# A fused encoder block on one core: the first gate and up blocks of the second feed-forward layer in alternating fours of halves, and the last quarter of x turned by VectorE

## What is computed

```python
def rms_norm(x, w):
    y = xf * lax.rsqrt(jnp.mean(xf * xf, axis=-1, keepdims=True) + EPS)
    return (y * w)

def swiglu(h, w_gate, w_up, w_down):            # 2048 -> 5632 -> 2048
    return (jax.nn.silu(h @ w_gate) * (h @ w_up)) @ w_down

x = x + 0.5 * swiglu(rms_norm(x, norm_ffn1_w), ...)
x = x + head_group_mixer(rms_norm(x, norm_mix_w), ...)
x = x + 0.5 * swiglu(rms_norm(x, norm_ffn2_w), ...)
return rms_norm(x, norm_final_w)
```

## Time and profile before

| | us |
|---|---|
| median of three runs | 1797.8 |
| the profiled execution | 1797.76 |
| its span in the trace | 1795.9 |
| PE busy | 1786.4 |
| VectorE busy | 1271.0 |
| ScalarE busy | 811.8 |

### The profile page before, as it was taken

The page is one execution under the profiler, slowest core; times in us unless marked ns, Lnnn a source line. Parts: engine busy times, 40 slices in busy tenths (PEclk is TensorE's granted clock), DMA queues, the critical chain, the costliest instruction groups (busy, mean ns, idle before and its releaser), DMA issues.

```text
span 1795.9 us, 22263 instructions
## 1 busy us (share of the span) xinstructions
PE 1786.4 (99%) x8104; PEld 1476.3 (82%) x8104; DVE 1271.0 (71%) x1622; ACT 811.8 (45%) x976; POOL 59.2 (3%) x57
## 2 busy tenths in 40 slices
PE   9999999999999999999999999999999999999998
PEld 7888888888888888888888888888888888888886
DVE  6676676676676678688888786676676667667668
ACT  6434444444443444555455445443443443444444
POOL 0000000000000000002222000000000000000000
PEclk9999999999999999999999999999999999999999
DMA  9655565565555555555546456556556556655552
GB/s 382 206 187 190 198 195 187 190 199 195 187 191 199 193 187 193 182 168 190 183 163 211 141 181 217 193 199 193 187 192 200 192 187 192 200 192 187 193 200 97
DMA packets 175590, 346.66 MB, mean 193 GB/s; under 512 B 5952, under 2 KB 8640, under 8 KB 175424
## 3 DMA queue, kind: packets, MB, share of 16 engines
q1 hardware_dynamic: 174976, 345.35, 57.8%
q10 hardware_dynamic: 576, 0.81, 0.1%
HBM read 344.04 MB, written 2.10 MB: 193 GB/s over the span
## 4 chain that ended last, share of the span: by engine, by line
PE 98%; DMA 0%; ACT 0%; issue 0%; DVE 0%; SPq 0%; POOLq 0%; POOL 0%; DVEq 0%; ACTq 0%
PE ps L381 32%; PE ps L382 32%; PE ps L383 32%; PE ps L410 0%; DMA raw<-in_g 0%; PE ps L598 0%; PE ps L587 0%; PE ps L523 0%; PE ps L536 0%; ACT w_hi L656 0%; PE ps L487 0%; PE ps L486 0%; PE ps L485 0%; SPq L337 0%; ACT xT_hi L663 0%
## 5 line engine op out<-in xcount | busy, mean ns | idle before, releaser
L901 DVE TENSOR_TENSOR w_lo<-raw,w_hi 128x1024 fp32r<-128x1024 f32 x644 | 797.3, 1239 | 496.7 <-ACT w_hi L679 495.3
L679 ACT ACTIVATE w_hi<-raw 128x1024 fp32r<-128x1024 f32 x644 | 681.3, 1059 | 955.6 <-PE ps L383 948.8
L381 PE MATMUL ps<-w_hi,xT_hi 128*128 128x512 f32 (+1 forms) x1808 | 702.2, 388 | 0.3 <-DVE xT_lo L934 0.3
L382 PE MATMUL ps<-w_lo,xT_hi 128*128 128x512 f32 (+1 forms) x1808 | 700.2, 387 | 0.0
L383 PE MATMUL ps<-w_hi,xT_lo 128*128 128x512 f32 (+1 forms) x1808 | 700.0, 387 | 0.0
L381 PEld LDWEIGHTS ps<-w_hi,xT_hi 128*128 128x128 f32 x1808 | 339.5, 188 | 71.2 <-issue 1.4
L383 PEld LDWEIGHTS ps<-w_hi,xT_lo 128*128 128x128 f32 x1808 | 339.5, 188 | 69.6
L382 PEld LDWEIGHTS ps<-w_lo,xT_hi 128*128 128x128 f32 x1808 | 339.6, 188 | 68.5
L383 PE MATMUL ps<-w_hi,hT_lo 128*128 128x512 f32 x640 | 249.0, 389 | 0.0
L381 PE MATMUL ps<-w_hi,hT_hi 128*128 128x512 f32 x640 | 249.0, 389 | 0.0
L382 PE MATMUL ps<-w_lo,hT_hi 128*128 128x512 f32 x640 | 249.0, 389 | 0.0
(11 more groups left out here) (116 smaller groups left out, 540.0 us busy)
## 6 DMA issues: line engine op xcount, KB each, us to landing
raw<-in_u SPq DMA_DIRECT2D x88, 1024.0 KB, 5.1
raw<-in_d SPq DMA_DIRECT2D x88, 1024.0 KB, 4.9
raw<-in_g SPq DMA_DIRECT2D x85, 1024.0 KB, 5.1
raw<-in_w_in SPq DMA_DIRECT2D x40, 1024.0 KB, 4.9
raw<-in_w_out SPq DMA_DIRECT2D x16, 1024.0 KB, 5.0
raw<-in_g SPq DMA_DIRECT2D x4, 512.0 KB, 7.6
x<-in_x SPq DMA_DIRECT2D x4, 512.0 KB, 12.8
raw<-in_w_in SPq DMA_DIRECT2D x4, 512.0 KB, 3.7
```

What stands on the lines that cost most here:

```text
L381: pe.matmul(out, xh, wh, start=first and j == 0, stop=False)
L382: pe.matmul(out, xh, wl, start=False, stop=False)
L679: act.activation(w_hi[:, k % LEAD, :, 0:width], words[:, :, 0:width], ACT.Copy).then_inc(hi_ready, 1)
L901: dve.tensor_tensor(w_lo[:, k % LEAD, :, 0:width], words[:, :, 0:width], f32(w_hi[:, k % LEAD, :, 0:width]), ALU.subtract).then_inc(lo_rea ...
```

## The change

The first gate and up blocks of the second feed-forward layer are no longer computed one after the other. The 16 halves go in fours: gate with pairs 0 to 3, up with pairs 0 to 3, gate with pairs 4 to 7, up with pairs 4 to 7 (`first_both`). The loads follow that order. Gate is complete behind half 11, so SiLU moves to position 13. Pair 4 is first used by half 8 where it was half 4, pair 6 by half 10 where it was half 6.

Quarter 3 is turned by VectorE in place of PE, four pieces behind each of positions 2 to 5 (`FOURTH_X`), into PSUM banks 6 and 7. ScalarE and VectorE write their parts of pairs 6 and 7 together ahead of position 7 (`LATER_PARTS`).

```diff
-X_BY_DVE = [(FFN2, 0), (FFN2, 2)]
+X_BY_DVE = [(FFN2, 0), (FFN2, 2), (FFN2, 3)]
+FOURTH_X = {2: (0, 4), 3: (4, 8), 4: (8, 12), 5: (12, 16)}
+FIRST_PARTS = {1: (4,), 2: (5,), 3: (6,), 4: (7,)}
+LATER_PARTS = {1: (4,), 2: (5,), 7: (6, 7)}
...
         def x_bank(norm, p):
-            return (0, 1, 2, 3, 4, 5, 2, 3)[p]
+            return p if norm == FFN2 else (0, 1, 2, 3, 4, 5, 2, 3)[p]
...
                     for s in range(4):
-                        if 4 * part + s >= loaded:
+                        if f == 1 and isinstance(i, int):
+                            load(g + part, s, rows(ffn_w[f][s // 2], 4 * P * (2 * part + s % 2), i * W))
+                        elif 4 * part + s >= loaded:
                             load(g + part, s, rows(ffn_w[f][part], 4 * P * s, i * W))
...
                     half(g, k, xT_hi, xT_lo, 2 * k, bank, k == 0, k == 7)
-                    if norm == FFN2 and bank == B_GATE and k in (2, 3):
-                        turn_x(norm, k + 4)
+
+            def first_both(g):
+
+                for pos in range(16):
+                    p, bank = 4 * (pos // 8) + pos % 4, (B_GATE, B_UP)[pos % 8 // 4]
+                    if bank == B_GATE:
+                        pe.wait_ge(xT_lo_ready, PAIRS * FFN2 + p + 1)
+                    half(g + pos // 8, pos % 8, xT_hi, xT_lo, 2 * p, bank, p == 0, p == 7)
...
             def silu(f, g, i):
-                act.wait_ge(half_used, 8 * g + 8)
+                act.wait_ge(half_used, 8 * g + (12 if f == 1 and isinstance(i, int) else 8))
...
                 for k in range(16):
-                    if 1 <= k < 5:
-                        xT(norm, k + 3)
+                    for p in (FIRST_PARTS, LATER_PARTS)[f].get(k, ()):
+                        xT(norm, p)
                     position(g0, k)
...
-                    if k == (13 if f == 0 else 9):
+                    if k == 13:
                         act.wait_ge(rstd_ready, (FFN1, FFN2)[f] + 1)
                         silu(f, g0, 0)
...
                 for k in range(16):
-                    if 1 <= k < 5:
-                        xT((FFN1, FFN2)[f], k + 3)
+                    for p in (FIRST_PARTS, LATER_PARTS)[f].get(k, ()):
+                        xT((FFN1, FFN2)[f], p)
                     position(g0, k)
+                    if f == 1 and k in FOURTH_X:
+                        turn_x(FFN2, 3, *FOURTH_X[k])
```

More of the change, by code:

```diff
@@ L440, in wide @@
                         continue
-                    if norm is not None and bank == B_GATE:
-                        pe.wait_ge(xT_lo_ready, PAIRS * norm + k + 1)
+                    if norm == FFN1 and bank == B_GATE:
+                        pe.wait_ge(xT_lo_ready, k + 1)
                     half(g, k, xT_hi, xT_lo, 2 * k, bank, k == 0, k == 7)
-                    if norm == FFN2 and bank == B_GATE and k in (2, 3):
-                        turn_x(norm, k + 4)
+            def first_both(g):
[4 more added lines that the diff above has]
+                    half(g + pos // 8, pos % 8, xT_hi, xT_lo, 2 * p, bank, p == 0, p == 7)
             def down(f, g, i):
@@ L490, in ffn @@
             def ffn(f):
-                norm = (FFN1, FFN2)[f]
-                wide(norm, G_FFN[f], B_GATE)
-                wide(norm, G_FFN[f] + 1, B_UP)
                 if f == 0:
+                    wide(FFN1, G_FFN[f], B_GATE)
+                    wide(FFN1, G_FFN[f] + 1, B_UP)
                     pe.wait_ge(ident_loaded, 16)
+                else:
+                    first_both(G_FFN[f])
                 def step(i):
```

## The result

The changed kernel takes 1802.93 us in the median of eight runs (1801.03 to 1804.11), the kernel before 1797.8 (1797.42 to 1798.38): the ratio is 1.0027, with a 95% interval of 1.0019 to 1.0036. It is 5.1 us slower, where 1797.6 was predicted. The profiled execution took 1801.29 us with a span of 1799.5, so it is one of the two quickest of the eight.

What follows compares the result with a forecast made beforehand. PE bounds the kernel, busy 1786.4 of 1795.9 us. Transposes removed, -0.99, plus the wait at half 10, +0.74, give -0.25 us from the profiled 1797.76: 1797.5, predicted as 1797.6 us; range 1796.6 to 1798.6.

Steps and rivals of the forecast that it cites:

- Edits at nothing: First block's later SiLU, reordered loads, squares and alternating PSUM banks cost nothing; SiLU has 3 us left before half 16.
- Gain: Second layer's start: eight transposes leave PE, saving 0.99 us, bounds 0.70 to 1.0.
- The wait at half 10: PE waits for pair 6's low parts near 1096: 0.61 us late plus 0.13 restart, 0.74 us in all.
- the higher value for a group: VectorE's four turned pieces take 1.91 us until the next split starts, not 1.77, in all four groups.
- The net of -0.25 us: Sum for the whole kernel: -0.99 for the transposes and +0.74 for the wait at half 10.
- the narrow place: Half 4: its split ends at 1079.49, PE asks at 1079.80; 0.3 us left, bound 0 to 0.15 lost.
- The loads: SyncE's loads come in another order at the same size, with at least 5 us of slack at each slot.
- A late load or a late split: Rival: a load in the way costs whole microseconds, up to a landing's 5.3 us: 1800 to 1803 us; chance 0.03.
- Slower by that much: Whole kernel slower by about 0.2%, 3.6 us, which needs the late load; chance 0.02.

Runs made afterwards that it cites:

- e3: e1 with quarter 3 turned by PE again, four transposes behind each of halves 2 and 3, in the alternating order; 1797.53 us, ratio 1.0.
- e2: The kernel before with one edit: SiLU of the second layer's last block waits for 12 used halves in place of 8; 1803.53 us, ratio 1.0032.
- e1: The changed kernel, but only the first block's SiLU waits for 12 halves, the last block's for 8 again; 1797.33 us, ratio 0.9999.
- e8: e4 with the first block's last eight halves in twos, loads following, and its SiLU waiting for 14 halves; 1796.76 us, ratio 0.9994.
- e4: e1 with each new group's four pieces in the order of input quadrants 1, 2, 3, 0 instead of 0, 1, 2, 3; 1796.88 us, ratio 0.9996.
- e6: e2 with 11 used halves in place of 12; 1798.99 us, ratio 1.0007.
- e5: e1 with gate's eight halves ahead of up's again and parts of pairs 6 and 7 written ahead of position 6; 1810.32 us, ratio 1.0069.

## Why the prediction was wrong

**The step that failed** is "Edits at nothing. SiLU moves from position 9 to 13: it can start when half 13 is used". I read `8 * g + (12 if f == 1 and isinstance(i, int) else 8)` as the first block's condition and put its term at nothing. In the first block that is so (e3). The same line also holds for the block written out behind the loop. I had asked what waits behind SiLU in the first block, and not in which calls the condition is true. Its price is 3.85 us where the clock stays (the changed kernel's profile) and 6.5 us where it falls (e2's profile), and it is the whole loss (e1). What the loss is made of could have been counted from the trace of before: half 12's split is queued behind SiLU on ScalarE.

**The first block was right.** Gain: 0.99 us forecast. The changed kernel's trace has no transposes of x there, and e8, which has the gain without a wait, is 0.94 us under the kernel before by the medians. The wait at half 10: 0.61 us late forecast, 0.61 measured, its restart 0.13. The choice of the higher value for a group by the last piece's quadrant was right, and e4 shows the quadrant to be the cause. That the sum is met to 0.01 us (12.56 against 12.55) is partly luck: the pieces took 1.85 to 1.93 us a group, 7.54 in all where 4 x 1.91 = 7.64 was forecast, and the splits ahead of them 5.01 where 4.92 was. The net of -0.25 us became -0.35 in e1. Half 4, called the narrow place, had no wait. The loads were in time.

**The rivals.** "A late load or a late split" gave a few whole microseconds, and I gave it 3% by looking at the loads' slack alone. It named the right kind of event, a split that comes late, but at the wrong place and with no mechanism. That the measured 1802.93 lies in its 1800 to 1803 is luck, since that price was the 5.3 us of a landing. "Slower by that much" had 0.02 and happened. The range of 1796.6 to 1798.6 held e1, that is the kernel I had in mind, and not the one that was changed. Nor did I price a fall of the granted clock, since the waits that I saw were under a microsecond.

## What to carry to other kernels

- Where a condition tests the kind of a loop index (a register or an integer), list every call for which it holds. A first and a last block written out around a loop look the same to it.
- A wait moved on an engine that also feeds a pipeline costs the work between the wait and the next thing asked of it, less what is still queued on the engine that asks. Here 3.7 us less 5.4, 2.7 and 0 us gave nothing, 1.0 and 3.7.
- Where one engine is busy 99% of the time, read every changed line for all of the span. A gain of one microsecond in one block is lost by one wait 640 us later.

## What the runs showed of the hardware

- In PE's wait of 3.7 us the granted clock fell to 1.2 GHz in e2's profile and stayed there for 13 matmuls, 2.8 us with the restart; it did not fall in the changed kernel's profile in the same wait. In 0.85 us (e6) and 0.45 us (e1) of shown idle time it stayed at 2.4 GHz; in 10.4 us (e5) it fell, and nine matmuls, 2.0 us, were paid. So the price of the same wait is not one number: 3.85 us or 6.5.
- A split (a VectorE instruction from partition 0 on) that follows a turned piece starts 0.08 to 0.10 us ahead of the piece's end if the piece read from the first quadrant (e4), and 0.02 to 0.03 behind it if it read from the last (the changed kernel). In all that was 12.03 against 12.55 us for four groups. The Trainium skill (VectorE: DVE Perf Modes, Two Vector instructions with no wait between them) says that an instruction starts only when every earlier one has finished if its first input from a memory starts in another quadrant than the input last read from that memory, or its output in another than the output last written there. e4 agrees: its last pieces wrote quadrants 0 to 3 of PSUM, the split reads and writes SBUF, and none of the four splits waited. The prediction gives the rule in short, without the memory.
